# Attention values of two heads multiplied together, alternating between the halves of a PSUM bank

## What is computed

```
def memory_attention(q, mem_k, mem_v):
    logits = einsum("bshd,bmhd->bhsm", qh, kh) * (HEAD_DIM ** -0.5)
    p = softmax(logits)
    o = einsum("bhsm,bmhd->bshd", p, vh)

def forgetting_attention(q, k, v, cum_logf):      # 12 heads, blocks of 128 queries
    logits = einsum("bqhd,bkhd->bhqk", qb, kb) * scale
    logits = logits + cum_logf[query] - cum_logf[key], causal mask
    o = einsum("bhqk,bkhd->bqhd", softmax(logits), vb)
```

## Time and profile before

| | us |
|---|---|
| median of 3 runs | 1257.6 |
| lowest, highest | 1256.13, 1257.68 |
| span of the profiled execution | 1251.5 |
| PE busy | 1209.8 (97%) |
| DVE busy | 894.0 (71%) |
| ACT busy | 639.7 (51%) |

### The profile page before, as it was taken

The page is one execution under the profiler, slowest core; times in us unless marked ns, Lnnn a source line. Parts: engine busy times, 40 slices in busy tenths (PEclk is TensorE's granted clock), DMA queues, the critical chain, the costliest instruction groups (busy, mean ns, idle before and its releaser), DMA issues.

```text
span 1251.5 us, 19242 instructions
## 1 busy us (share of the span) xinstructions
PE 1209.8 (97%) x7928; PEld 1092.5 (87%) x7928; DVE 894.0 (71%) x1369; ACT 639.7 (51%) x1017; POOL 14.0 (1%) x32
## 2 busy tenths in 40 slices
PE   6999899999999999999999999999999999999997
PEld 6988798999989869899998978878798989999885
DVE  5996678877776666788778856665576647677664
ACT  6564555555464435555555334435444555555553
POOL 0000000000000000000000000000000000000000
PEclk9999999999999999999999999999999999999999
DMA  9520435555443323465454544544454732223341
GB/s 387 220 101 1 168 135 174 213 186 187 183 169 123 105 86 126 157 214 198 174 201 137 205 164 157 205 168 146 173 186 174 259 147 102 102 102 102 135 178 58
DMA packets 28710, 200.52 MB, mean 160 GB/s; under 512 B 3408, under 2 KB 3536, under 8 KB 5072
## 3 DMA queue, kind: packets, MB, share of 16 engines
q1 hardware_dynamic: 28624, 199.30, 43.8%
HBM read 198.24 MB, written 1.05 MB: 159 GB/s over the span
## 4 chain that ended last, share of the span: by engine, by line
PE 80%; DVE 11%; ACT 5%; issue 3%; DMA 1%; DVEq 0%; POOLq 0%; ACTq 0%; POOL 0%; SPq 0%
PE bank L726 22%; PE bank L727 22%; PE bank L728 22%; DVE WL L1616 4%; ACT WH L1236 3%; PE bank L874 2%; DVE work L1808 2%; PE bank L1210 1%; PE bank L1193 1%; PE bank L1107 1%; PE bank L860 1%; DVE work L1761 1%; DVE work L1757 1%; PE bank L937 1%; PE bank L1184 1%
## 5 line engine op out<-in xcount | busy, mean ns | idle before, releaser
L1616 DVE TENSOR_TENSOR WL<-RAW,WH 128x2048 fp32r<-128x2048 f32 x180 | 411.5, 2289 | 151.2 <-ACT WH L1236 150.1
L1236 ACT ACTIVATE WH<-RAW 128x2048 fp32r<-128x2048 f32 x180 | 343.2, 1910 | 208.5 <-PE bank L728 202.8
L726 PE MATMUL bank<-XH,WH 128*128 128x256 f32 x1264 | 361.9, 286 | 18.1 <-DVE WL L1828 12.0
L727 PE MATMUL bank<-XL,WH 128*128 128x256 f32 x1264 | 358.6, 284 | 0.0
L728 PE MATMUL bank<-XH,WL 128*128 128x256 f32 x1264 | 358.5, 284 | 0.0
L726 PEld LDWEIGHTS bank<-XH,WH 128*128 128x128 f32 x1264 | 243.4, 193 | 22.5 <-DVE XL L1821 11.9
L727 PEld LDWEIGHTS bank<-XL,WH 128*128 128x128 f32 x1264 | 243.4, 193 | 0.5
L728 PEld LDWEIGHTS bank<-XH,WL 128*128 128x128 f32 x1264 | 243.4, 193 | 0.0
L726 PE MATMUL bank<-WH,MH 128*128 128x512 f32 (+1 forms) x544 | 199.7, 367 | 5.7 <-DVE WL L1616 3.8
L727 PE MATMUL bank<-WL,MH 128*128 128x512 f32 (+1 forms) x544 | 196.7, 362 | 0.0
L728 PE MATMUL bank<-WH,ML 128*128 128x512 f32 (+1 forms) x544 | 196.6, 361 | 0.0
(11 more groups left out here) (275 smaller groups left out, 1507.0 us busy)
## 6 DMA issues: line engine op xcount, KB each, us to landing
RAW<-wstream SPq DMA_DIRECT2D x181, 1024.0 KB, 4.8
con<-consts SPq DMA_DIRECT2D x1, 1681.0 KB, 13.2
work<-xT_in SPq DMA_DIRECT2D x1, 1024.0 KB, 4.9
x<-x_in SPq DMA_DIRECT2D x1, 1024.0 KB, 11.0
work<-mem_in SPq DMA_DIRECT2D x1, 1024.0 KB, 16.3
xn<-memT_in SPq DMA_DIRECT2D x1, 1024.0 KB, 11.9
par<-params SPq DMA_DIRECT2D x1, 858.0 KB, 14.2
gfree<-g_final SPq DMA_DIRECT2D x1, 512.0 KB, 17.0
```

Of the source, the lines that this page charges most:

```text
L726: mm(o, ah, bh, start=start, stop=False)
L727: mm(o, ah, bl, start=False, stop=False)
L1236: act_fn(WH[:, t % RING, :], RAW[:, t % RING, :], ACT.Copy).then_inc(w_rounded, 1)
L1616: tt(WL[:, t % RING, :], RAW[:, t % RING, :], WH[:, t % RING, :].bitcast(F32), ALU.subtract).then_inc(w_split, 1)
```

## The change

The values of an even head are no longer multiplied in their own slot. In the odd head's slot a new function `values` multiplies both: for each half of the keys first the even head's matmul, then the odd head's. The bank `("O", h)` is taken in that slot too, so that its place in ring B is one slot later. PE waits for both heads' copies of the probabilities at once, and `probT` has three buffers in place of two.

```
             if 0 <= s - 2 < n:
                 aux("B", ("T", base + s - 2), "dve")
-            if 0 <= s - 3 < n:
-                if (s - 3) % 2 == 0:
-                    u.append(("B", ("O", base + s - 3), "dve_values", "later"))
-                else:
-                    u.append(("complete", [("O", base + s - 4)], None, None))
+            if 0 <= s - 3 < n and (s - 3) % 2 == 1:
+                aux("B", ("O", base + s - 4), "dve_values")
...
-        probT = wk(6656, 2, 512)
+        probT = wk(6656, 3, 512)
...
-                    if 0 <= s - 3 < n:
-                        u = s - 3
-                        if u % 2 == 0:
-                            o_val = take(("O", base + u))
+                    if 0 <= s - 3 < n and (s - 3) % 2 == 1:
+                        u = s - 4
+                        o_val = take(("O", base + u))
                         if units[u][0] == "fox" and u % 4 == 0:
                             is_free(pe, ("v1", u // 4))
-                        pe.wait_ge(*pt_a.next())
-                        last = value(units[u], o_val, probT[:, u % 2, :])
-                        if u % 2 == 1:
-                            last.then_inc(aux_done, 1)
+                        pe.wait_ge(*pt_a.next(2))
+                        values([(units[v], probT[:, v % 3, :]) for v in (u, u + 1)], o_val).then_inc(aux_done, 1)
...
+            def values(pair, o):
+
+                for j in range(TT):
+                    for (kind, *l, h), pt in pair:
+                        r = slice(DH * (h % 2), DH * (h % 2) + DH)
+                        if kind == "mem":
+                            last = mm(o[r, 0:T], mvv[:, l[0], j, DH * h:DH * (h + 1)], pt[:, j * T:(j + 1) * T],
+                                      start=(j == 0), stop=(j == TT - 1))
+                        else:
+                            last = mm(o[r, j * P:T], v1[:, j, DH * h:DH * (h + 1)], pt[:, j * T:j * P + T],
+                                      start=(j == 0), stop=(j == TT - 1))
+                return last
...
-                        copy(probT[:, (s - 2) % 2, 0:w], B(("T", base + s - 2))[:, 0:w]).then_inc(pt_done, 1)
+                        copy(probT[:, (s - 2) % 3, 0:w], B(("T", base + s - 2))[:, 0:w]).then_inc(pt_done, 1)
```

## The result

| | before | changed |
|---|---|---|
| median of 10 runs each, us | 1256.3 | 1249.6 |
| lowest to highest | 1253.5 to 1258.0 | 1245.4 to 1254.9 |
| span of the profiled execution | 1251.5 | 1243.8 |

The ratio is 0.9945, with a 95% interval of 0.9929 to 0.9961: the change makes the kernel 0.55% faster. The forecast was 1252.4, with a range from 1249.4. Against the 1257.6 that the forecast started from, the ratio gives 1250.7.

A forecast was written before the change was run, and what follows sets the result against it. TensorE (PE), busy for 97% of the span, was taken as the bound. Gains of 1.77 + 3.10 - 0.22 + 0.77 - 0.22 = 5.2 us took 1257.6 to 1252.4, range 1249.4 to 1258.2.

The forecast's parts named there:

- the first part of the mechanism: Both attentions: the way into and out of 64-column matmuls, 0.236 us (memory) or 0.342 (forgetting), is paid once per pair.
- The step that failed: Value matmuls of a pair: in-order starts allow partial overlap, memory pair 5u instead of 8u, forgetting pair 4u instead of 6u.
- The rival of full overlap: Value matmuls: both halves stream fully side by side, gaining 7.15 us, so 1250.5; chance 0.22.
- The partial overlap that I forecast: Value matmuls of both attentions: the halves overlap in part, gaining 5.2 us, so 1252.4; chance 0.36.
- The places where nothing is gained: Second attention: pairs 8/9 and 14/15 at PE's waits cost 0.22 us each, pair 12/13 gains nothing.
- The wait behind the first attention: Before L1018: PE's wait stays at 1.1 us, so what PE gains in the first attention passes through.
- The drain per change of half: Value matmuls: each change of half costs 0.17 us, three per pair, giving 1261.5, slower; chance 0.12.
- The case without overlap: Value matmuls: only the ways in and out are saved, 0.7 us in sum, so 1256.9; chance 0.24.
- The third buffer, the bank order, the odd slots: Attention slots: probT's third buffer and later bank are worth nothing; a wait in odd slots, 0.99 us shorter, would refute.
- The clock: Granted clock falls over 122 to 128 us: half speed costs 1.7 us; the shift may blur the result by that.

The follow-up runs named there:

- e5: As the changed kernel, but both heads write to output rows 0 to 63, through one half of the array; ratio to the kernel before 1.0002.
- e2: As the changed kernel, but not alternated: both matmuls of the even head, then both of the odd head; ratio to the kernel before 0.9939.

## Why the prediction was right or wrong

- **The direction and the first part of the mechanism were right.** The way into and out of the 64-column matmuls is paid once per pair: in e5, without overlap, a memory pair adds 99.59 - 97.19 - 0.44 = 1.96 us between transposes and taps, where two single heads added 2 x 1.10. That saves 0.24, and 0.236 was forecast. It is the small part of the gain; the large part is the overlap.
- **The step that failed** is "PE starts its instructions strictly in order ... but the second instruction of one head can run beside the first of the other". It put a memory pair's streaming at 5u and a forgetting pair's at 4u. Measured from L942's start to the next line's, a memory pair takes 1.01 us, as much as one head, so its streaming is 4u; a forgetting pair takes 0.80 us, against 0.79 for one head, so it is 3u. I had read the order of starts from rows in which all instructions used the same half, or the whole array; they could not show what happens across halves. The row that I gave for weight loads under running matmuls is the start of L952's matmul, not of its load; that the loads overlap is right all the same. The rival of full overlap, which got 0.22, was the true case, and the terms of the sum are its terms: 2.20 forecast there against 2.39 for the first attention, 3.96 against 3.97 up to slot 11, 0.99 against 0.96 behind o1. The 1250.5 that it gave fits the 1250.7 by the ratio. The partial overlap that I forecast had the right sign and 5.2 of about 7 us, for a reason that does not hold.
- **The range**, from 1249.4, ended one microsecond below the full-overlap case. Both the median, 1249.6, and the 1250.7 by the ratio lie inside it, near its lower end: it holds them because the rival was let in, not because the forecast's mechanism was right. The microsecond for clock and spread was too little. The four fastest of the ten executions (1245.4 to 1246.1 us) have a mean granted clock of 0.995, the three slowest (1253.2 to 1254.9) one of 0.988, and 0.007 of the span is 8.7 us: nearly all of the spread is the clock.
- **The places where nothing is gained were right.** From slot 11's transposes to o1 it is 3.19 us in both traces: the values taken from slot 11 only lengthened the wait. The last head's values begin 7.98 us after slot 15's transposes, against 7.89 before. But the wait before o1 grew to 2.7 us where "near 2.9" stood, and that before the last pair to 2.6 where "over 1.5" stood.
- **The wait behind the first attention** stayed at 1.1 us, so that all of its gain passed through, as worked out from VectorE's idle 3.29 us.
- **The drain per change of half** did not appear: two instructions of different halves start together. The case without overlap, on which that rival was built, is what e5 shows when both heads use one half.
- **The third buffer, the bank order, the odd slots:** no wait appeared at any of them. That they are worth nothing is supported by e5, which has them all and ties with the kernel before.
- **The clock** I had left as a blur of 1.7 us that the shift might cause. In the profiled execution the fall at 123 us was gone (1.5 us gained) and one at 460 us came (1.6 us lost). Over all executions the change moved the loss to the clock by less than can be measured.

The Trainium skill had the true case. TensorE: Matmul & The Clock Gate, Part 3, gives a packed group the span of one matmul plus some nanoseconds per tile; 1.01 us for two heads and for one agrees. Two other sentences of that section the runs contradict: that matmuls start strictly in the order of the queue (e2 lasts 1.02 us, which an in-order start would make at least 7u = 1.5), and that weight loads overlap running matmuls only in another row group (both halves here use all rows, and all eight loads of a pair lie within its 1.01 us, while its matmuls stream).

## What to carry to other kernels

The 64-column matmuls of this kernel cost half as much when those for one half of the output partitions stand close to those for the other half in the queue, with no wait between; they need not alternate. Before packing, ask which of them already run in a wait, because those gain nothing and only lengthen it. Then look at the order of work of the engine that is waited for: moving VectorE's maxima and weight split behind what TensorE waits for gave a further 3.3 to 3.9 us, half of what the change gave. And where executions of one kernel spread, compare their mean granted clocks before you compare medians: here that explains nearly all of the 9 us.

## What the runs showed of the hardware

- The two halves run fully side by side in these float32 matmuls: eight instructions of 256 columns in 1.01 us, against 1.87 through one half.
- A later matmul for the other half passes earlier ones that wait for their own half: over three instructions in e2.
- At the two waits that the change lengthens, the granted clock fell to half (1.2 of 2.4 GHz) in seven of ten cases after PE idled for 2.4 us or more, and in none of ten after 1.9 us or less. Elsewhere a wait of 1.6 to 1.7 us was followed by a fall in six of ten profiles, so this is no threshold.
- The mean granted clock of an execution, 0.988 to 0.995 for the changed kernel, accounts for nearly all of the 9 us between its executions.
